# Experts of a two-layer decoder step: slots found ahead of the loop, gated rows added in DRAM, last normalisation by rows

## What is computed

```python
def _moe(x, w_router, w_exp_gu, w_exp_down):
    logits = (x @ w_router).astype(jnp.float32)
    top_v, top_i = lax.top_k(logits, TOP_K)
    gates = jax.nn.softmax(top_v, axis=-1)
    gate = jnp.sum(jax.nn.one_hot(top_i, N_EXPERTS, dtype=jnp.float32) * gates[..., None], axis=-2)
    out = jnp.zeros_like(x)
    for e in range(N_EXPERTS):
        out = out + _swiglu(x, w_exp_gu[e], w_exp_down[e]) * gate[..., e:e + 1].astype(x.dtype)
    return out
```

## Time and profile before

| | |
|---|---|
| Median of 3 runs | 1794.18 us (1792.43 to 1798.73) |
| Profiled execution: its span, first to last instruction | 1790.7 us |
| PE busy | 1743.2 us, 97%, 8760 matmuls |
| DVE busy | 1214.5 us, 68% |
| ACT busy | 845.4 us, 47% |
| POOL busy | 111.8 us, 6% |
| HBM read, written | 444.97 MB, 13.46 MB |
| Mean DMA rate over the span | 257 GB/s |

### The profile page before, as it was taken

How to read it: one execution, slowest core, us unless ns; L and a number is a source line. 1 busy time by engine, 2 the same in 40 slices (tenths; PEclk the granted TensorE clock), 3 DMA queues, 4 the chain that set the end, 5 groups by cost and what they waited for, 6 DMA issues and landing times.

```text
span 1790.7 us, 23663 instructions
## 1 busy us (share of the span) xinstructions
PE 1743.2 (97%) x8760; PEld 1362.3 (76%) x8760; DVE 1214.5 (68%) x1659; ACT 845.4 (47%) x898; POOL 111.8 (6%) x120
## 2 busy tenths in 40 slices
PE   7999999999999999999999999999999999999998
PEld 4646487689999574558677888888888888888886
DVE  2687635255544287552715989899898989898994
ACT  1122211144442122212204777777777777777774
POOL 0630000000000252000001000000000000000000
PEclk9999999999999999999998999999999999999999
DMA  9556554855424445663672989899998989898980
GB/s 321 189 201 213 217 188 153 287 171 188 166 94 178 156 162 199 218 229 135 242 258 72 349 298 381 335 380 338 372 394 315 392 318 387 320 384 336 379 321 26
DMA packets 218514, 459.32 MB, mean 257 GB/s; under 512 B 10878, under 2 KB 49976, under 8 KB 218422
## 3 DMA queue, kind: packets, MB, share of 16 engines
q1 hardware_dynamic: 212710, 442.63, 68.3%
q0 software_dynamic: 3424, 11.50, 2.0%
q10 hardware_dynamic: 2304, 4.20, 0.6%
HBM read 444.97 MB, written 13.46 MB: 256 GB/s over the span
## 4 chain that ended last, share of the span: by engine, by line
PE 85%; DVE 7%; ACT 4%; issue 1%; DMA 1%; SPq 1%; POOL 0%; ACTq 0%; DVEq 0%; POOLq 0%
PE bank L1228 83%; PE bank L1232 3%; DVE arena L2701 1%; DVE ring_low L2170 1%; ACT high L1784 1%; DMA out<-mem_rows 1%; DVE R L2315 1%; ACT L1784 1%; ACT arena L1855 0%; POOL arena L972 0%; ACT ye_high L1823 0%; ACT SQ L1876 0%; DVE st L2673 0%; DVE st L2594 0%; SPq L734 0%
## 5 line engine op out<-in xcount | busy, mean ns | idle before, releaser
L2170 DVE TENSOR_TENSOR ring_low<-ring,high 128x2048 fp32r<-128x2048 f32 x264 | 598.7, 2288 | 81.3 <-ACT high L1784 80.5
L1784 ACT ACTIVATE high<-ring 128x2048 fp32r<-128x2048 f32 x264 | 505.1, 1918 | 141.8 <-PE bank L1228 137.6
L1228 PE MATMUL bank<-high,xg_high 128*128 128x512 f32 x704 | 278.1, 395 | 7.3 <-DVE ring_low L2170 7.0
L1228 PE MATMUL bank<-ring_low,xg_high 128*128 128x512 f32 x704 | 274.6, 390 | 0.0
L1228 PE MATMUL bank<-high,xg_low 128*128 128x512 f32 x704 | 274.2, 389 | 0.0
L1228 PEld LDWEIGHTS bank<-high,xg_high 128*128 128x128 f32 x704 | 132.2, 188 | 34.7 <-DVE ring_low L2170 8.4
L1228 PEld LDWEIGHTS bank<-ring_low,xg_high 128*128 128x128 f32 x704 | 132.2, 188 | 28.0
L1228 PEld LDWEIGHTS bank<-high,xg_low 128*128 128x128 f32 x704 | 132.3, 188 | 25.7
L1855 ACT ACTIVATE arena<-bank 128x512 f32<-128x512 f32 (+3 forms) x95 | 46.3, 525 | 217.1 <-PE bank L1228 141.5
L1228 PE MATMUL bank<-high,he_high 128*128 128x512 f32 x352 | 140.0, 398 | 0.0
L1228 PE MATMUL bank<-ring_low,he_high 128*128 128x512 f32 x352 | 137.4, 390 | 0.0
(11 more groups left out here) (327 smaller groups left out, 2578.0 us busy)
## 6 DMA issues: line engine op xcount, KB each, us to landing
ring<-in_w_exp_gu SPq DMA_DIRECT2D x176, 1024.0 KB, 9.9
ring<-in_w_exp_down SPq DMA_DIRECT2D x40, 2048.0 KB, 10.5
ring<-in_w_in SPq DMA_DIRECT2D x12, 2048.0 KB, 11.2
ring<-in_w_ffn_gu SPq DMA_DIRECT2D x22, 1024.0 KB, 8.7
ring<-in_w_ckv SPq DMA_DIRECT2D x8, 2048.0 KB, 9.1
ring<-in_cache_mem_k SPq DMA_DIRECT2D x16, 1024.0 KB, 8.1
ring<-in_cache_mem_v SPq DMA_DIRECT2D x16, 1024.0 KB, 6.6
ring<-in_cache_attn_k SPq DMA_DIRECT2D x32, 256.0 KB, 3.9
```

The source lines that it names most:

```text
L1228: return M.matmul(out, lhsT, rhs, start=start, stop=stop)
L1784: S.activation(high_bufs[h % HIGH_BUFS][:], ring[:, s, j * HALF:(j + 1) * HALF], ACT.Copy).then_inc(split_high, 1)
L2170: V.tensor_tensor(ring_low[:, s, part], ring[:, s, part], high_bufs[h % HIGH_BUFS][:], ALU.subtract).then_inc(split_low, 1)
```

## The change

The scatter by matmuls, the turned selection matrix and the column accumulator `acc` are gone. All slots' tokens and gates are found once, ahead of the loop: selection matrices for all experts (DVE makes experts 0 to 3, POOL 4 to 7), and 24 PE matmuls of two columns each, of which one gives the slot's row and the other its gate (`slots_by_product`, `slots` on DVE). The layer's sum lies as token rows in DRAM (`y_rows`: 128 rows that take what empty slots send, then 264). POOL scales `x_tok` by alpha and stores it there, and ACT's loop waits until this has landed, since the scaled rows lie where the experts' hidden values will. At the end of an expert DVE alone multiplies the result by the gates (`ye`, in plain 32 bits), and POOL adds the 128 rows to `y_rows` by an indirect DMA that accumulates. On POOL's queue the gather for expert e+2 now stands behind the addition of expert e. Behind the loop SP reads the rows back, DVE finds mean and variance by row (`bn_stats`, `bn_aggr`), ACT the root, DVE normalises with gain and shift that SP has loaded to all partitions, and SP stores. POOL's memsets ahead of the routing are no longer behind a scaling.

The diff, cut to its core:

```diff
+            sp.dma_start(gain_row, a["ln_g"][L - 1, 2].partition_broadcast(P)).then_inc(norm_rows_landed, 16)
+            for h in range(2):
+                sp.dma_start(shift_row[h], a["ln_b"][L - 1, 2, 512 * h:512 * (h + 1)].partition_broadcast(P)
+                             ).then_inc(norm_rows_landed, 16)
...
+            sp.wait_ge(y_rows_written, rows_written(EXPERTS, 0))
+            for t, (t0, n) in enumerate(TILES):
+                sp.dma_start(y_tok[0:n, t, :], y_rows[P + t0:P + t0 + n, :]).then_inc(y_landed[t], 16)
...
-                    xT_act.wait(pool, l, 13)
-                    xT_dve.wait(pool, l, 1)
-                    for k in range(KT):
-                        G.tensor_scalar(acc[:, k, :], xT[:, k, :], ALPHA, None, ALU.mult).then_inc(part_added, 1)
                     G.memset(x_tok[:, 2, :], 0.0).then_inc(buffers_set, 1)
-                    G.memset(gates[:], 0.0).then_inc(buffers_set, 1)
+                    G.memset(slot_vals, 0.0).then_inc(buffers_set, 1)
                     G.memset(posp[:], -1.0).then_inc(buffers_set, 1)
+                    copied(pool, (l, "xtok", 5))
+                    for t, (_, n) in enumerate(TILES):
+                        G.tensor_scalar(first_rows[0:n, t, :], x_tok[0:n, t, :], ALPHA, None, ALU.mult
+                                        ).then_inc(rows_scaled, 1)
+                    for t, (t0, n) in enumerate(TILES):
+                        pool.wait_ge(rows_scaled, t + 1)
+                        pool.dma_start(y_rows[P + t0:P + t0 + n, :], first_rows[0:n, t, :]
+                                       ).then_inc(y_rows_written, 16)
...
+            def add_rows(e, c):
+
+                pool.wait_ge(y_by_dve, results_before(e + 1, c))
+                pool.wait_ge(y_rows_written, rows_written(e, c))
+                pool.indirect_dma_start(
+                    out=y_rows, out_offset=bass.IndirectOffsetOnAxis(ap=slot_row[0:lots, e:e + 1], axis=0),
+                    in_=ye[0:lots, :], in_offset=None, bounds_check=P + T - 1, compute_op=ALU.add
+                ).then_inc(y_rows_written, 16)
+
             def one_pass(c):
+                pool.wait_ge(slots_in, c + 1)
+                for e in range(EXPERTS // 2, EXPERTS):
+                    for t in range(3):
+                        ins = G.tensor_scalar(Sel[:, e, t, 0:lots], iota[:, 0:lots], posp[:, t, e:e + 1], None,
+                                              ALU.is_equal)
+                    ins.then_inc(pool_sel_ready, 1)
+                pool.wait_ge(slots_known, 2 * (c + 1))
                 for e in range(EXPERTS):
                     gather_rows(e, c)
+                    add_rows(e, c)
 
...
+            def slots_by_product(c):
+
+                pe.wait_ge(slots_in, c + 1)
+                if c:
+                    pe.wait_ge(y_by_dve, results_before(EXPERTS, c - 1))
+                for e in range(EXPERTS):
+                    if e < EXPERTS // 2:
+                        pe.wait_ge(sel_ready, EXPERTS // 2 * c + e + 1)
+                    else:
+                        pe.wait_ge(pool_sel_ready, EXPERTS // 2 * (c - 1) + e + 1)
+                    for t in range(3):
+                        last = mm(Y_BANKS[0][0:lots, 2 * e:2 * e + 2], Sel[:, e, t, 0:lots], slot_vals[:, t, e, :],
+                                  t == 0, t == 2)
+                last.then_inc(slots_full, 1)
...
                 for f in range(NGU):
                     gate_up(f)
-                    if 2 * f < KT:
-                        scatter_before(f)
                     if f and f % 2 == 0:
                         transpose_h(f // 2 - 1)
                 down(0)
                 transpose_h(PAIRS - 1)
...
                 down(1)
-                scatter_matrix()
                 down(2)
...
-                gather_by_product(0, c)
-                warm(T_BANKS[0], 3)
+                gather_by_product(c)
+                slots_by_product(c)
                 with pe.Fori(0, EXPERTS) as e:
                     expert(e, c)
-                last_scatter(c)
...
-                    if p == NGU + 3:
-                        act.wait_ge(scatter_full, i + 1)
-                        S.activation(slot_gate[0:lots], T_BANKS[0][0:lots, 3 * P:3 * P + 1], ACT.Copy).then_inc(gate_ready, 1)
-                        S.activation(SelT[0:lots, :], T_BANKS[0][0:lots, 0:T], ACT.Copy).then_inc(scatter_ready, 1)
-                take_gathered(x_groups_before(e, c) + KT)
+                take_gathered(x_groups_before(e, c))
...
                 act.wait_ge(dn_done, i * NDN + NDN)
-                act.wait_ge(gate_ready, i + 1)
-                for n in range(2):
-                    S.activation(ye_high[0:lots, n, :], Y_BANKS[n][0:lots, :], ACT.Copy, scale=slot_gate[0:lots]
-                                 ).then_inc(y_by_act, 1)
...
             act.wait_ge(pos_known, 1)
+            act.wait_ge(y_rows_written, rows_written(0, 0))
             most = act.value_load(cnti[0:1, 0:1], min_val=0, max_val=T)
             one_pass(0)
...
                 dve.wait_ge(dn_done, i * NDN + NDN)
+                dve.wait_ge(y_rows_written, rows_written(e, c))
                 for n in range(2):
-                    dve.wait_ge(y_by_act, 2 * i + n + 1)
-                    V.scalar_tensor_tensor(ye_low[n][0:lots], Y_BANKS[n][0:lots, :], slot_gate[0:lots],
-                                           ye_high[0:lots, n, :], ALU.mult, ALU.subtract).then_inc(y_by_dve, 1)
...
+                    V.tensor_scalar(ye[0:lots, 512 * n:512 * (n + 1)], Y_BANKS[n][0:lots, :],
+                                    slot_gates[0:lots, bass.ds(e, 1)], None, ALU.mult).then_inc(y_by_dve, 1)
+            def slots(c):
+
+                found = Y_BANKS[0][0:lots, 0:2 * EXPERTS].rearrange("p (e n) -> p e n", n=2)
+                dve.wait_ge(slots_full, c + 1)
...
+                V.tensor_scalar(slot_at[0:lots], found[:, :, 0], -1.0, const[0:lots, C_TOK:C_TOK + 1], ALU.mult, ALU.add
+                                ).then_inc(slot_steps, 1)
+                V.tensor_copy(slot_gates[0:lots], found[:, :, 1]).then_inc(y_by_dve, 1)
+                dve.wait_ge(slot_steps, c + 1)
+                V.tensor_copy(slot_row[0:lots], slot_at[0:lots]).then_inc(slots_known, 1)
+                V.tensor_scalar(slot_token[0:lots], slot_at[0:lots], -float(P), 0.0, ALU.add, ALU.max
+                                ).then_inc(slots_known, 1)
+                dve.wait_ge(y_by_dve, results_before(0, c))
...
+                selection(0)
+                token_of = const[:, C_TOK:C_TOK + 3].unsqueeze(2).to_broadcast([P, 3, EXPERTS])
+                V.scalar_tensor_tensor(slot_vals[:, :, :, 0], posp[:, :, 0:EXPERTS], -float(P), token_of,
+                                       ALU.add, ALU.subtract).then_inc(slots_in, 1)
+                for e in range(1, EXPERTS // 2):
+                    selection(e)
                 low_part(0, c, 0)
                 low_of_gathered((2 * EXPERTS + 2) * c, x_groups_before(0, c) - 2)
+                slots(c)
                 with dve.Fori(0, EXPERTS) as e:
                     expert(e, c)
-                last_scatter(c)
...
+                    def row_moments(t):
+
+                        n = TILES[t][1]
+                        dve.wait_ge(y_landed[t], 16)
+                        for h in range(2):
+                            V.bn_stats(row_stats[0:n, t, 6 * h:6 * h + 6], y_tok[0:n, t, 512 * h:512 * (h + 1)]
+                                       ).then_inc(y_stats, 1)
+                        dve.wait_ge(y_stats, 2 * t + 2)
+                        V.bn_aggr(moments[0:n, t, 0:2], row_stats[0:n, t, :]).then_inc(y_moments, 1)
+
+                    def normed_rows(t):
+
+                        n = TILES[t][1]
+                        dve.wait_ge(y_moments, t + 1)
+                        for h in range(2):
+                            part = y_tok[0:n, t, 512 * h:512 * (h + 1)]
+                            V.scalar_tensor_tensor(part, part, moments[0:n, t, 0:1], gain_row[0:n, 512 * h:512 * (h + 1)],
+                                                   ALU.subtract, ALU.mult).then_inc(y_half, 1)
+                        dve.wait_ge(y_rstd, t + 1)
+                        for h in range(2):
+                            part = y_tok[0:n, t, 512 * h:512 * (h + 1)]
+                            dve.wait_ge(y_half, 2 * t + h + 1)
+                            V.scalar_tensor_tensor(part, part, moments[0:n, t, 2:3], shift_row[h][0:n, :],
+                                                   ALU.mult, ALU.add).then_inc(y_ready, 1)
+
+                    dve.wait_ge(norm_rows_landed, 16 * 3)
+                    row_moments(0)
+                    for t in range(3):
+                        if t < 2:
+                            row_moments(t + 1)
+                        normed_rows(t)
```

More of the change, by code:

```diff
@@ L302, in psum_groups @@
             add("V", "pos")
-        add("V", "mu", 2)
-        add("A", "var", 2)
-    for n in range(6):
```

(7 more changed lines are left out.)

184 lines of the change are left out of this document (59 added, 125 removed).

## The result

| | before | after |
|---|---|---|
| median of the runs | 1794.45 us (4 runs, 1792.43 to 1798.73) | 1767.74 us (4 runs, 1765.79 to 1770.88) |
| ratio | | 0.9846, 95% interval 0.9829 to 0.9863 |
| span of the profiled execution | 1790.7 us | 1764.0 us |
| first product of the loop to the end of its last | 978.14 to 1763.00: 784.9 us | 981.47 to 1736.85: 755.4 us |
| a middle expert | 98.23 us | 94.27 us |

What follows compares the result with a forecast made beforehand. TensorE was taken to bound the kernel (85% of the chain that ended last), DMA close behind. -29.6 + 2.0 + 1.6 - 0.5 = -26.5 gave a span of 1764.2, with 3.5 more 1767.7 us; range 1760 to 1782.

Steps and rivals of the forecast that it cites:

- The matmuls that leave TensorE: Expert loop: scatter matmuls, next tokens' passes and the selection matrix's turn leave TensorE's path, saving 1.44, 0.59 and 0.91 us per expert.
- The other two pieces: Expert loop, TensorE: six passes for the next tokens, 0.59 us, and the selection matrix's turn with its gate column, 0.91.
- The gap: Expert's start, third half of the weights: ACT's scaling leaves the chain TensorE waits for, gaining 0.8 of its 1.29 us.
- The loop as a whole: All eight experts: 3.74 us gained in each of seven and 3.42 in the first, together -29.6 us.
- The addition: Expert loop: one accumulating DMA per expert costs 1.4 to 4.2 us, hidden in 3.6 free, so counted as nothing.
- The rival that each row pays a round trip of 1.3 us: Expert loop: the addition holds the DMA engines, 10.4 us per expert, time about 1815 us; 6%.
- Ahead of the loop: Before the first expert: slot products behind the first gather start the loop at 980.1 against 978.14, +2.0 us, up to 2.6.
- ACT's new wait: Ahead of the loop: ACT waits for scaled rows in DRAM, starting about 971 instead of 965.81, covered with 1.6 us left.
- The clock: First expert's start: the narrow slot products bring the 1.2 GHz level, charged as half of 3.2 us, +1.6.
- the Trainium skill's page as rival: First expert's start: only idle gaps lower the clock, so the 1.6 us are not paid, giving 1766 us; 20%.
- Behind the loop: After the last expert: multiply, last addition, load, DVE's normalising and store end at 1790.2, -0.5 us; bounds -3 and +5.
- The 3.5 from span to median: Whole kernel: the median of the runs, 1794.18 us, stands 3.5 above the profiled span, 1790.7; added to the forecast span.

Runs made afterwards that it cites:

- run 20: No label: the words are "in this run 20 us", a duration. That run: changed kernel with table set loaded once, slot products mixed into the gather, two fillers; 1768.32 us.

## Why the prediction was right

**The matmuls that leave TensorE** (1.44 + 0.59 + 0.91). Right: the sixteen cost 1.43 when they are put back. The other two pieces were not tried by themselves; a middle expert gained 3.96 where 3.74 was predicted, and with 1.43 and 0.86 measured 1.67 is left for what was reckoned at 1.50. The 0.17 stand in the starts on either side of the pieces, which the step left out. Before, the two transposes ahead of the six passes, and the second product behind the turn; then the same transposes now, and the product behind them:

```profile
1440.84 0.38 PE L1232 MATMUL bank<-const,arena 128*128 128x128 f32 x2
...
1448.41 0.40 PE L1228 MATMUL bank<-high,he_low 128*128 128x512 f32 x1
```

```profile
1333.96 0.38 PE L1231 MATMUL bank<-const,arena 128*128 128x128 f32 x2
1334.10 0.48 PE L1227 MATMUL bank<-high,he_high 128*128 128x512 f32 x1
```

The pair took 1441.06 - 1440.84 = 0.22 and takes 0.14 now. The first product behind the turn took 1448.41 - 1448.10 = 0.31 where a product takes 0.23, and this went with the turn. Together they make 0.16.

**The gap** (0.8 per expert). Right: 0.86, and the scaling on ACT is its cause. The 0.5 us for ACT's return to the loop's head stood on no row; ACT's table load began 1.49 us behind the expert's first product (1469.65) and begins 0.59 behind it now, so of the 1.29 us of scaling 0.39 are taken up again and 0.90 are gone. What the step did not say is that the rest of the gap hung on the table load next in that chain; without it the gap is gone. An idle time that is read off a timeline understates such a gap: 0.61 of idle time was worth 0.93.

**The loop as a whole** (-29.6). Measured -29.5 (784.9 to 755.4). That includes the clock in the first products, which the prediction had as a term of its own: nine starts in 981.47 to 985.20, 0.41 us apart on average instead of 0.23, 1.7. At full clock the loop gained 31.2.

**The addition** (nothing, 1.4 to 4.2 of engine time, 3.6 free). Right that it is hidden: without it an expert lasts 94.27 all the same. The price is 2.7, close to the 2.8 by the sentence of the Trainium skill and not the 1.4 of a plain transfer. The free time was sized too small: about 3 us remain with the addition in. By these counts, without additions an expert needs 99.3 - 4 x 2.7 = 88.5 us of the engines, or 95.5 - 2.7 - 3 x 1.3 = 88.9, and not the 90.9 that 387 GB/s gave. What an expert needs is read from a run that is short of it. The rival that each row pays a round trip of 1.3 us falls: additions land after 9 us and take 2.7 us of the engines' time.

**Ahead of the loop** (+2.0, at most 2.6). Missed by 1.4: the loop starts at 981.47, not at 980.1. Of this 0.3 is the router, which began at 954.14 for 953.82 in work that no edit touches. From there to the gather it is 16.23 us for 16.59, so 0.36 of the 0.46 were gained. The selection products wait no more, but PE's wait ahead of the fillers, ended by no other engine, is 2.13 us, and it was 1.57. The slot products took 981.47 - 970.37 - 6.06 = 5.0 us, where 4.1 was taken and 4.7 was the other bound: 0.9, the term that was too small. The nearest row was one with 8 columns, and passes of two columns are no cheaper. ACT's new wait came as reckoned (969.27 for 971), covered by the slot products.

**The clock** (+1.6, with the Trainium skill's page as rival). Measured 1.7. The section that the prediction names there warns of idle gaps; in the runs the unbroken row of narrow passes was followed by 1.2 GHz, or ran into it, and 1.10 us of idle time behind mixed passes was not.

**Behind the loop** (-0.5). Right in the sum, by errors that cancel: from the end of the multiplication the addition took 7.2 us and not 5.6 (0.8 to its issue, 6.4 from there to the load of the rows), the load 3.9 and not 3.6, DVE 12.2 and not 13.5, the last store about 2.2 and not 3.0 (it is that of the 8 rows).

The span came out at 1764.0 for 1764.2 predicted: the start's 1.4 too much is made good by the 1.6 that the loop gained beyond the forecast. That the time fell within 0.3 us of the forecast is luck in part. The mechanisms were right, but two errors of about 1.5 us cancelled, and so did those of the tail. The 3.5 from span to median held too (3.7 now), since both profiled spans lie as far below the fastest run of their kernel, 1.7 and 1.8.

## What to carry to other kernels

A DMA that is added to a loop close to the DMA's limit is costed in engine time, not in time to landing: double or quadruple it, and read the queue's share and the lengthened period. Where a chain of short steps ends an engine's idle time, look at every step of it; here a table load that a missing preload put at the head of each iteration was worth 0.93 us, and the edit's own gain there was 0.86. Before fillers ahead of narrow matmuls are shortened, read the granted clock behind them: a gather that started 2.6 us sooner made the kernel 9 us slower.

## What was not expected of the hardware

- With two filler products ahead, the 96 passes of gather and slot products ran unbroken for 20.3 us at a granted 0.50; with five, the same passes ran at 1.00 but for their first microsecond. The Trainium skill ("TensorE: Matmul & The Clock Gate", section "What's actually happening") has the clock follow how busy the array has been; in this run 20 us of unbroken work did not raise it.
- An accumulating DMA of 128 rows of 4 KB takes 2.7 us of the time of all 16 engines, a plain one of the same rows 1.3. The page's line on bytes read from HBM, 447.10 MB, is the same with 8 and with 32 additions, so the second read does not stand there.
- POOL's `TENSOR_TENSOR` on 8 partitions slowed DVE's instructions on 128 partitions to more than double (3.14 us for 1.40).
